# Branch-gate blocks of a two-layer hybrid decoder trunk dealt 6, 3, 5, 2 to the four mixers instead of 5, 2, 5, 4

## The reference, cut to what matters

```python
proj = h @ w_in[l]
(hq, hf, hi, hg, mcq, mckv, mkr, dq, dk, dv, sq, sk, sv, gates) = jnp.split(proj, SPLIT_POINTS, axis=-1)
y_a = hgrn2_mixer(...); y_b = mla_mixer(...); y_c = diff_mixer(...); y_d = swa_mixer(...)
branch = jnp.einsum('bsnw,nwd->bsnd', ys, w_branch[l])
gate = jax.nn.sigmoid(gates.reshape(B, S, N_BRANCH, D))
merged = jnp.sum(gate * branch, axis=2)
x = x + gt1[:, None, :] * (merged @ w_out[l])
```

## Time and profile before

| | |
|---|---|
| median of three runs | 2330.77 us |
| the profiled execution, own time | 2330.08 us |
| its span in the trace | 2328.4 us |
| mean granted TensorE clock | 0.978 |
| TensorE matmul busy | 2175.7 us, 93% |
| VectorE / ScalarE / GpSimd busy | 64% / 43% / 16% |
| share of TensorE in the chain that ended last | 74% |

### The profile page before, as it was taken

The page is one execution under the profiler, slowest core; times in us unless marked ns, Lnnn a source line. Parts: engine busy times, 40 slices in busy tenths (PEclk is TensorE's granted clock), DMA queues, the critical chain, the costliest instruction groups (busy, mean ns, idle before and its releaser), DMA issues.

```text
span 2328.4 us, 32683 instructions
## 1 busy us (share of the span) xinstructions
PE 2175.7 (93%) x12027; PEld 1722.1 (74%) x12027; DVE 1485.6 (64%) x2691; ACT 1008.5 (43%) x1859; POOL 377.8 (16%) x346
## 2 busy tenths in 40 slices
PE   7999988999899999999999999989998999999996
PEld 5897877787677786777669878777866778777774
DVE  5637765635655876777646487667265569467775
ACT  4523334534455334555435333345344553345552
POOL 2002200000000341444300121000000014214451
PEclk9999999999999999999999999999999999999998
DMA  9322222232223865766642222421322357446663
GB/s 302 91 85 70 90 91 91 69 96 65 80 86 106 288 227 228 295 236 238 198 144 88 81 75 91 126 74 33 114 60 76 98 190 257 181 178 257 242 217 118
DMA packets 196573, 333.71 MB, mean 143 GB/s; under 512 B 30528, under 2 KB 153280, under 8 KB 180416
## 3 DMA queue, kind: packets, MB, share of 16 engines
q1 hardware_dynamic: 169184, 305.33, 38.8%
q0 software_dynamic: 19296, 19.98, 2.7%
q10 hardware_dynamic: 7936, 6.30, 0.8%
HBM read 352.48 MB, written 51.38 MB: 173 GB/s over the span
## 4 chain that ended last, share of the span: by engine, by line
PE 74%; DVE 11%; ACT 6%; DMA 4%; issue 4%; SPq 1%; POOL 0%; POOLq 0%; ACTq 0%; DVEq 0%
PE ps L874 69%; PE ps L872 5%; DVE spare L2072 2%; DVE ring_rounded L2090 2%; ACT WH_rounded L1583 1%; DVE ssq L2257 1%; DVE nmax L2314 1%; DMA SQKV<-gate_logits 1%; DMA ring<-in_w_in 1%; DMA DVt<-gate_logits 1%; DMA Y<-in_ada_w 1%; ACT SC L1719 1%; DMA Y<-y_rows 1%; DVE ps L2311 1%; DVE SC L2681 0%
## 5 line engine op out<-in xcount | busy, mean ns | idle before, releaser
L874 PE MATMUL ps<-X_rounded,WH_rounded 128*128 128x512 f32 x768 | 340.9, 444 | 18.8 <-ACT CM L1631 6.5
L2090 DVE TENSOR_TENSOR ring_rounded<-ring,WH_rounded 128x512 fp32r<-128x512 f32 (+2 forms) x190 | 235.0, 1245 | 173.4 <-ACT WH_rounded L1583 173.1
L874 PE MATMUL ps<-H_rounded,WH_rounded 128*128 128x512 f32 x768 | 305.5, 398 | 8.3 <-DVE SC L2681 8.3
L874 PE MATMUL ps<-X_rounded,ring_rounded 128*128 128x512 f32 x768 | 304.6, 397 | 0.0
L874 PE MATMUL ps<-WH_rounded,X_rounded 128*128 128x256 f32 (+1 forms) x960 | 276.9, 288 | 17.7 <-issue 15.6
L874 PE MATMUL ps<-ring_rounded,X_rounded 128*128 128x256 f32 (+1 forms) x960 | 274.2, 286 | 0.0
L874 PE MATMUL ps<-WH_rounded,H_rounded 128*128 128x256 f32 (+1 forms) x960 | 274.0, 285 | 0.0
L3023 POOL TENSOR_TENSOR M<-M,SC 128x512 f32<-128x512 f32 x48 | 75.8, 1592 | 1044.7 <-DVE SC L2681 1044.7
L1583 ACT ACTIVATE WH_rounded<-ring 128x512 fp32r<-128x512 f32 (+2 forms) x190 | 195.2, 1037 | 98.8 <-PE ps L874 62.7
L874 PEld LDWEIGHTS ps<-X_rounded,WH_rounded 128*128 128x128 f32 x768 | 146.7, 191 | 91.1 <-issue 44.1
L874 PEld LDWEIGHTS ps<-WH_rounded,X_rounded 128*128 128x128 f32 x960 | 187.6, 195 | 21.6 <-issue 18.9
(11 more groups left out here) (396 smaller groups left out, 4495.8 us busy)
## 6 DMA issues: line engine op xcount, KB each, us to landing
ring<-in_w_in SPq DMA_DIRECT2D x272, 256.0 KB, 4.0
Y<-in_moe_w_down SPq DMA_DIRECT2D x18, 1024.0 KB, 6.7
ring<-in_ada_w SPq DMA_DIRECT2D x64, 256.0 KB, 4.9
ring<-in_w_branch SPq DMA_DIRECT2D x64, 256.0 KB, 5.2
TM<-in_ada_w SPq DMA_DIRECT2D x14, 1024.0 KB, 10.3
DQK<-in_ada_w SPq DMA_DIRECT2D x14, 1024.0 KB, 9.0
ring<-in_moe_w_down SPq DMA_DIRECT2D x14, 1024.0 KB, 6.1
gate_logits<-CM SPq DMA_DIRECT2D x44, 256.0 KB, 2.9
```

The source lines that it names most:

```text
L874: ins = nc.tensor.matmul(o, lhsT, rhs, start=start, stop=stop)
L2090: ins = v.tensor_tensor(low[j][:, at:at + size], ring[:, j, at:at + size], high[i][:, at:at + size].bitcast(F32), ALU.subtract)
```

## The change

It deals the 16 gate blocks of a layer 6, 3, 5, 2 over HGRN2, MLA, diff and SWA, takes away the own rule of `share` for HGRN2 (the even one gives it 3 steps in each of its 32 units), and moves the ring order and the split times accordingly: MLA's third gate block is loaded behind ("ada", 14) and ("ada", 15) and split from unit 15 on, ("d", 0) from unit 24 in place of 18; in the SWA sweep two splits remain, of gate block 15 from unit 1 and of ("branch", 0) from unit 18 in place of 26; `strewn` takes one block more.

```diff
-GATE_SLOTS = {"hgrn": 5, "mla": 2, "diff": 5, "swa": 4}
-FIRST_GATE = {"hgrn": 0, "mla": 10, "diff": 14, "swa": 24}
+GATE_SLOTS = {"hgrn": 6, "mla": 3, "diff": 5, "swa": 2}
+FIRST_GATE = {"hgrn": 0, "mla": 12, "diff": 18, "swa": 28}
@@
-              + [("c", 4), ("c", 5)] + ada_keys(3, 0) + gate_keys("mla")
-              + ada_keys(3, 2) + [("d", 0), ("d", 1), ("d", 2)] + gate_keys("diff") + gate_keys("swa")
+              + [("c", 4), ("c", 5)] + ada_keys(3, 0) + gate_keys("mla")[:2]
+              + ada_keys(3, 2) + gate_keys("mla")[2:] + [("d", 0), ("d", 1), ("d", 2)] + gate_keys("diff") + gate_keys("swa")
@@
-AFTER = {("c", 0): ("c", 2), ("hg_y", 0): ("c", 3), ("up", 0): ("c", 4), ("turn", 0): ("c", 5), ("turn", 2): ("gate", 5),
-         ("d", 0): ("d", 2), ("d", 1): ("gate", 7), ("d", 2): ("gate", 8)}
+AFTER = {("c", 0): ("c", 2), ("hg_y", 0): ("c", 3), ("up", 0): ("c", 4), ("turn", 0): ("c", 5), ("turn", 2): ("gate", 6),
+         ("d", 0): ("d", 2), ("d", 1): ("gate", 9), ("d", 2): ("gate", 10)}
@@
-IN_SWEEP = {"mla": quarters(1, {2: ("gate", 6), 18: ("d", 0)}),
-            "diff": quarters(2, {4: ("gate", 9), 7: ("gate", 10), 10: ("gate", 11), 13: ("gate", 12)}),
-            "swa": quarters(1, {1: ("gate", 13), 9: ("gate", 14), 17: ("gate", 15), 26: ("branch", 0)})}
+IN_SWEEP = {"mla": quarters(1, {2: ("gate", 7), 15: ("gate", 8), 24: ("d", 0)}),
+            "diff": quarters(2, {4: ("gate", 11), 7: ("gate", 12), 10: ("gate", 13), 13: ("gate", 14)}),
+            "swa": quarters(1, {1: ("gate", 15), 18: ("branch", 0)})}
@@
 def share(kind, n, units):
 
     steps = 2 * NC * GATE_SLOTS[kind]
-    if kind == "hgrn":
-        return tuple(min(steps, m // 3 * NC + (0, 3, 6)[m % 3]) for m in (n, n + 1))
     return steps * n // units, steps * (n + 1) // units
@@
-    for i, key in enumerate([("gate", 1), ("gate", 2), ("gate", 3), ("gate", 4), ("c", 0), ("c", 1)]):
+    for i, key in enumerate([("gate", i) for i in range(1, GATE_SLOTS["hgrn"])] + [("c", 0), ("c", 1)]):
```

## The result

The changed kernel took 2389.61 us, median of four runs, against 2332.26 us for the kernel before on the same chip (four runs, 2330.62 to 2334.18). The ratio is 1.0233, with a 95% interval of 1.021 to 1.0256: slower, and by 57 us where the prediction had 7. Three of the runs took 2383.75 to 2390.16 us at mean granted clocks of 0.953 and 0.954; the fourth took 2436.09 us at 0.933.

A forecast was written before the change was run, and what follows sets the result against it. TensorE, busy 93% of the span, was taken as the bound. Layer 1: 16.0 + 1.1 + 6.8 - 0.8 - 20.2 = +2.9; layer 2 +3.9; +6.8 on 2330.1 gives 2336.9, plus 0.7 for the median: 2337.6 us, range 2325 to 2350.

The forecast's parts named there:

- SWA, 64 steps to 32: SWA sweep: one step fewer in each of 32 units saves 22.1 us, two stalls cost 1.9: -20.2 us a layer.
- sign of a wrong step: Stage lengths that would prove a step wrong: HGRN2 under 126 us, or SWA over 70.
- clock at MLA's start: MLA's first gap shrinks to 2.7 us, perhaps avoiding a low-clock stretch: -0.8 us a layer, between 0 and -1.7.
- The price of a step, HGRN2: HGRN2, 80 steps to 96: steps 11.0, eight stops at chunk copies 8.0, less 3.0: +16.0 us a layer.
- The relief: HGRN2: of 3.3 us of gaps where VectorE is late, 3.0 us a layer go, bounds 0 and 3.3.
- Behind HGRN2: c projections: ScalarE does three split quarters before the norm instead of one, so TensorE waits +1.1 us, between 0 and 1.6.
- MLA: MLA sweep, 32 steps to 48: +6.8 and +7.8 us by layer; +6.0 and +7.0 with the clock at MLA's start.
- The clock in HGRN2: HGRN2: gaps up to 1.04 us brought no lower clock; the skill's rule would put 1.2 GHz behind eight new waits.
- Free waits in HGRN2: Rival: HGRN2's eight stops cost nothing, 8.0 us a layer go, 2321.6 us; chance 0.12.
- MLA for nothing: Rival: MLA's added steps fall into its idle time, giving back some 3.5 us a layer, about 2331 us; chance 0.20.
- SWA at its chain of 2.5 us: Rival: ScalarE or VectorE sets SWA's pace at 2.5 us a unit in three later tiles, 2354 us; chance 0.08.
- The clock falls behind the stops: Rival: HGRN2's 16 stops each bring 3.4 us at half clock, costing 1.7 each, +27, 2365 us; chance 0.04.

The follow-up runs named there:

- runs with doubled steps: Changed kernel with SWA gate steps issued twice: all 2384.65 us; units 4 and 5 2341.7; unit 4 2344.31; from unit 8 on 2380.78; every second from there 2372.3.
- aligned kernel: Changed kernel with HGRN2's 96 steps dealt so that each of the 12 chunks ends with a unit: 2372.83 us.
- units 4 and 5 doubled: Changed kernel with the gate steps of SWA units 4 and 5 alone issued twice: 2341.7 us, ratio 1.003 to the kernel before.
- unit 4 alone: Changed kernel with the gate step of SWA unit 4 alone issued twice: 2344.31 us, ratio 1.0034 to the kernel before.
- second profile: The kernel before, unedited, profiled once more: 2335.9 us, c projections 130.5 us in layer 1 and 124.9 in layer 2.
- other dealings: The changed kernel and follow-up kernels whose gate steps are dealt differently from the kernel before: c took 127.6 to 131.0 us in twelve profiles.

## Why the prediction was wrong, and where it was right

The sign was right and the size was not: 2337.6 us against 2389.61, far outside the range.

**The step that failed** is "SWA, 64 steps to 32": 22.1 us by matmul spacings taken at full clock, with +1.9 for two stalls in units 4 and 5. The stalls were seen, placed and priced at what they last. What they do to the clock was not asked. Its own sign of a wrong step, an SWA stage over 70 us, is there: 111.9. The prediction's own rows had the mechanism: a gap of 3.38 us followed by a low stretch of 3.4 us. From them it took that a fall ends after one such stretch, and it looked for the clock at MLA's start and at HGRN2's stops, where the gaps are. In SWA the gaps are far shorter than at MLA's start and about as long as HGRN2's stops, but what follows them is the thinnest filler of the kernel, and there the clock didn't come back for a hundred us. The runs with doubled steps show both halves: with both stalls filled, or the first alone, no fall, with more steps behind them a fall that ends after 14 to 17 us. What decides which sweep falls stays open. It is not two independent throws: of the twelve runs of the changed and the aligned kernel eleven have just one fall, one has two and none has none, where two independent sweeps at about one half each would give a single fall in half of the runs. Something ties the two sweeps of an execution, and no run here shows what.

**The rest of the sum came out, in part by luck.** Without a fall the changed dealing is 7.8 us slower than the kernel before (units 4 and 5 doubled, same chip) or 6.7 us (unit 4 alone), with sweeps as long as the changed kernel's own. The sum said +6.8. The stages agree less well: without the 43.1 us of the fall the differences of the table add up to +5.7 and +10.1 us, where +2.9 and +3.9 were forecast, against a profiled execution that was faster than all four timed runs of the kernel before. The c stage is the term that was sized too small, by 3 to 4 us a layer.
- *The price of a step, HGRN2:* +16.0 forecast, +16.2 and +16.3 measured. A stop costs 1.0 us (0.94 and 0.09), as worked out. The relief was put at 3.0, and the aligned run shows its two parts: the added steps alone cost 9.7 us (125.1 against 115.4) and not 11.0, the stops 6.5 and not 8.0, so 1.3 and 1.5, 2.8 together.
- *Behind HGRN2:* the gap ahead of the second c projection grew from 3.35 to 4.55 us, 1.2 where 1.1 was forecast. The row of the changed kernel that answers to the earlier trace rows:

```profile
314.64 0.55 PE L872 MATMUL ps<-WH_rounded,X_rounded 128*128 128x256 f32 x1 [4.55 <-issue]
```

- The remaining 3 to 4 us of c are low clock: 0.93 and 0.96 in the changed kernel's c stages against 0.97 and 0.99. The kernel before shows it too in one layer of its second profile; that it is more frequent with the other dealings is not explained.
- *MLA:* +6.0 and +7.0 forecast; +4.0 and +8.8 measured. The stage mostly has one of two lengths: 85.6 to 86.4 us where TensorE's gap at the start is 1.56 to 1.63 us, and 90.1 (twice 87.5) where it is 2.70, with more low clock behind it. The changed kernel's layers are one of each. The prediction took the gap to be 2.7 and the clock to cost 0.8 us; both of these vary from one execution to the next, and the term is right only between the two. TensorE's stall at the weights of d 0 is gone, as forecast: ScalarE still waits 1.4 us for that load, and nobody for ScalarE.
- *SWA, layer 1:* -20.2 forecast, -20.4 measured.
- *The clock in HGRN2:* eight stops of 0.7 to 0.8 us in each layer at a clock of 1.00, and a stage of 131.6 or 131.7 us in all sixteen layers profiled with these stops. The rule cited from the Trainium skill, page "TensorE: Matmul & The Clock Gate", section "A second HAM failure mode: psum-queue depth-cycling", is not borne out by these stops: the trace doesn't agree there.

**The rivals.** Free waits in HGRN2: refuted. MLA for nothing: refuted, a little more was hidden than thought in one layer. SWA at its chain of 2.5 us: refuted, full-clock units last as long as TensorE's work. "The clock falls behind the stops" had the right kind and the wrong place, with 4% and 2365 us; it too reckoned with 3.4 us for each fall.

## What to carry to other kernels

Filler did two things here: it used idle time, and where it was dense a fallen clock came back. When a change thins a stage, don't cost its short stalls by their own length; ask what the stage would take if the clock fell there and stayed, and give that case a chance of its own. The cure was cheap: the same steps, dealt so that the two stalls are filled and HGRN2's chunks end with units, turned a kernel 2% slower into one 0.2% faster, though that gain is only just clear of the noise. And steps that wait on one buffer belong at a boundary where other work covers the copy: 6.5 us a layer for a dealing table.

## What the hardware did that was not expected

- TensorE stayed at 1.2 GHz for the last 99.6 us of a sweep while it was busy for 97.7 of them, and in another execution for 96.7 us while busy for all of them. With one gate step a unit it stayed low to the end of the sweep, with 1.5 and with 2 it returned, and behind the sweep it returned some 3 us into the merge's matmuls of 128x512.
- The same sweep without a fall runs at 1.00 from end to end. One and the same work was held at either level.
- Stalls of 0.7 to 0.8 and 0.3 to 0.4 us that ended 2.3 us apart brought a fall in 13 of 24 sweeps, but in eleven of twelve runs in just one of the two; the second stall alone brought none in 16; eight stops of 0.7 to 0.8 us, 11 or 22 us apart, brought none in HGRN2; one of 1.58 us there brought a short one in one layer of two. The Trainium skill, "TensorE: Matmul & The Clock Gate", section "HAM oscillation — how this bites in real kernels", tells of a kernel in which DMA waits of some 3 to 5 us throttled the clock, so that the work behind each started slow. The trace agrees for the gap of 3.38 us at MLA's start; in SWA it differs, since none of the stalls lasts over 0.83 us.
- The same kernel's c stage differs by 5.6 us between two layers of one execution, with the granted clock at 0.92 or 0.99.
